# Prompt attention of a hybrid decoder step: scores made as query rows for the maximum and a second time with keys on the partitions for the exponential

## What is computed

```python
s = jnp.einsum('bqhd,bkhd->bhqk', qb, k) * scale
s = s + cq[..., :, None] - ckT[:, :, None, :]
s = jnp.where(kpos <= qpos, s, -jnp.inf)
p = jax.nn.softmax(s, axis=-1)
o = jnp.einsum('bhqk,bkhd->bqhd', p, v)
y = (o * jax.nn.silu(z)) @ w_out
```

## Time and profile before

| what | us |
|---|---|
| median of 3 runs (lowest, highest) | 2239.72 (2234.27, 2247.66) |
| the profiled execution's own time | 2248.77 |
| its span, first to last instruction | 2247.0 |
| first instruction of `attend` | 1391.8 from the span's start |
| first matmul of the output projection | 2116.1 |
| PE busy in the span | 1930.5 (86%) |

### The profile page before, as it was taken

One profiled execution on the slowest core, in us unless ns is written; L12 is line 12 of the kernel. 1 busy time (PEld: TensorE's weight loads), 2 busy tenths in 40 slices (PEclk: granted clock), 3 DMA queues, 4 the chain that ended last, 5 costly groups with the idle time before them and its releaser, 6 DMA issues. The chain is left out here.

```text
span 2247.0 us, 39897 instructions
## 1 busy us (share of the span) xinstructions
PE 1930.5 (86%) x15120; PEld 1416.0 (63%) x15120; DVE 1129.9 (50%) x1810; ACT 563.5 (25%) x1253; POOL 349.8 (16%) x401
## 2 busy tenths in 40 slices
PE   4999999999999788999999996877877768768798
PEld 3876877777787566877877774544444434344475
DVE  4444534544563687677677763333334333333423
ACT  4211121121121421111111111333433334233431
POOL 0000000000000034544445442011011010110010
PEclk9999999999999898999999997568889788687899
DMA  4111111111111479999999997247678676685761
GB/s 136 38 44 48 43 40 56 35 49 47 39 49 38 161 232 308 343 312 341 348 325 330 317 323 253 105 154 248 218 212 258 224 233 225 203 257 181 276 243 71
DMA packets 218393, 413.65 MB, mean 184 GB/s; under 512 B 18593, under 2 KB 129858, under 8 KB 218014
## 3 DMA queue, kind: packets, MB, share of 16 engines
q1 hardware_dynamic: 148764, 222.15, 30.6%
q0 software_dynamic: 51648, 180.71, 23.5%
q10 hardware_dynamic: 17874, 9.27, 1.4%
HBM read 370.85 MB, written 41.94 MB: 184 GB/s over the span
## 5 line engine op out<-in xcount | busy, mean ns | idle before, releaser
L1180 DVE STREAM_TRANSPOSE kt<-k_raw 128x1024 f32<-128x1024 f32 x256 | 310.8, 1234 | 145.7 <-DMA k_raw<-in_cache_k_dram,k_idx 120.0
L347 POOL DMA_INDIRECT k_raw<-in_cache_k_dram,k_idx x256 | 259.4, 1013 | 444.4 <-DVE kt L1180 284.6
L765 PE MATMUL ps_a<-h_hi,w_hi 128*128 128x512 f32 x656 | 265.7, 405 | 1.7 <-DVE w_lo L1017 1.7
L766 PE MATMUL ps_a<-h_lo,w_hi 128*128 128x512 f32 x656 | 258.7, 394 | 0.0
L767 PE MATMUL ps_a<-h_hi,w_lo 128*128 128x512 f32 x656 | 258.6, 394 | 0.0
L1693 DVE TENSOR_REDUCE pp_nm<-ps_a 128x1 f32<-128x128 f32 (+3 forms) x64 | 48.5, 758 | 306.4 <-PE ps_a L1421 306.4
L1017 DVE TENSOR_TENSOR w_lo<-w_raw,w_hi 128x1024 fp32r<-128x1024 f32 x97 | 109.1, 1124 | 171.3 <-ACT w_hi L594 169.0
L1443 PE MATMUL b<-con,p_p 128*128 128x128 f32 x432 | 98.4, 347 | 102.7 <-DVE p_p L1701 48.4
L765 PE MATMUL ps_b<-h_hi,w_hi 128*128 128x512 f32 x384 | 157.2, 409 | 0.0
L766 PE MATMUL ps_b<-h_lo,w_hi 128*128 128x512 f32 x384 | 152.1, 396 | 0.0
L767 PE MATMUL ps_b<-h_hi,w_lo 128*128 128x512 f32 x384 | 152.0, 396 | 0.0
(11 more groups left out here) (291 smaller groups left out, 3131.8 us busy)
## 6 DMA issues: line engine op xcount, KB each, us to landing
v_pg<-in_cache_v_dram SPq DMA_DIRECT2D x256, 512.0 KB, 5.1
w_raw<-in_w_in_pool_dram SPq DMA_DIRECT2D x32, 512.0 KB
w_raw<-in_w_in_attn_dram SPq DMA_DIRECT2D x32, 512.0 KB
w_raw<-in_w_out_pool_dram SPq DMA_DIRECT2D x16, 512.0 KB
s_scr<-ss_st ACTq DMA_DIRECT2D x64, 128.0 KB
s_in<-s_scr POOLq DMA_DIRECT2D x16, 512.0 KB, 5.0
d_sb<-decay POOLq DMA_DIRECT2D x32, 256.0 KB, 6.9
z_scr<-x_st SPq DMA_DIRECT2D x8, 528.0 KB, 4.6
```

The source lines that it names most:

```text
L347: pool.indirect_dma_start(k_raw[:, k, :], None, cache_rows, bass.IndirectOffsetOnAxis(ap=k_idx[:, u, k:k + 1], axis=0)).then_inc(k_full[k] ...
L765: nc.tensor.matmul(ps, ah, bh, start=j == 0, stop=False)
L766: nc.tensor.matmul(ps, ah, bl, start=False, stop=False)
L1180: V.transpose(kt[u % 2][:, :, 32 * k:32 * k + 32], k_raw[:, k, :].rearrange("p (i c) -> p i c", c=32)).then_inc(dve_kt, 1)
```

## The change

It touches `attend`, its buffers, and little else.

- The row maxima of a pair are made ahead of it. `query_rows(b+1, m)` computes the scores as before, for m = 0 to 7, in parts of at most 512 columns, spread over slots 1 to 6 of pair b; DVE takes each part's maximum (`row_max`), then the negated maxima of all 16 blocks in one tile (`max_columns`). PE transposes it (`max_turn`, slot 7), ACT copies it out, and ACT's own queue writes it to DRAM (`nm_d`, 8 KB) and, after that has landed, reads it into row 66 of `qa` (`max_row`). `k_aug` gets a row more that matches it.
- The scores are made a second time with the keys on the partitions: `keys_turned(b, s)`, key block s against all queries from block s on, minus the maximum. They and the row scores go through a ring of four PSUM banks. ACT's exponential writes straight to `pt_x`, two buffers for each head. No block is transposed, and none is normalised.
- `prompt_values` now takes up to 512 columns at a time and adds up all slots in `ps_a`. The sums over the keys are made by DVE (`part_sums`, adds of `pt_x` into `acc`) and by PE (`row_sums`, a matmul with ones, twice a pair). `gate` divides and multiplies twice a pair, 512 columns each.
- In a slot, the values of slot s-1 stand ahead of the turned scores of slot s; then come row scores, the sample's turn, and sample values.
- `qa`, `ka`, `v_pr` have two buffers. The queries, keys and values of pair b+1 are asked for when the turned scores and the values of pair b-1 are done; `score_half` two pairs ahead.
- The sample of pair b is done within pair b. All 8 pairs carry one, and the output projection carries none. Ahead of pair 0 stand its row scores, its sample scores and the first exchange of maxima. `w_o` is asked for early in the last pair.
- The gates are loaded in one transfer after the first sample scores.

The core of the diff:

```diff
+        ring = (ps_b[:, 0:512], ps_b[:, 512:1024], ps_c[:, 0:512], ps_c[:, 512:1024])
+        M_SLOTS = ((), (0, 1), (2,), (3, 4), (5,), (6,), (7,), ())
+        def turned(s):
+            return [(h, a, e) for h in range(2) for a, e in ((P * s, 512), (max(512, P * s), SEQ)) if a < e]
+        def row_parts(m):
+            return [(h, a, e) for h in range(2) for a, e in ((0, min(512, P * m + P)), (512, P * m + P)) if a < e]
...
+                def keys_turned(b, par, s, uses):
                     if s == 0:
-                        pe.wait_ge(ld_qk, b * 32 + 32)
+                        pe.wait_ge(ld_nm, b * 16 + 16)
+                    for i, (h, a, e) in enumerate(turned(s)):
+                        j = uses.index(("t", T_AT[s] + i))
+                        ring_wait(b, uses, j)
+                        diag = a == P * s
+                        out = ring[j % 4]
+                        mm = nc.tensor.matmul(out[:, 0:e - a], ka[par][:, h, P * s:P * s + P], qa[par][:, h, a:e],
+                                              start=True, stop=not diag)
+                        if diag:
+                            mm = nc.tensor.matmul(out[:, 0:P], caus_b[:, :], ident_b[:, :], start=False, stop=True)
+                        mm.then_inc(pe_t, 1)
...
+                def max_turn(b):
+                    pe.wait_ge(dve_nx, b + 1)
+                    pe.wait_ge(dve_s, b * N_S + 5)
+                    nc.tensor.transpose(b6[0:16, 0:P], nm_c[:, :], ident).then_inc(pe_nm, 1)
...
+                    for a, e in ((P * s, 512), (max(512, P * s), SEQ)):
+                        if a < e:
+                            for h in range(2):
+                                r = HD * h
+                                mm = nc.tensor.matmul(o_ps[r:r + HD, a:e], v_pr[par][:, s, r:r + HD], pt_x[h][s % 2][:, a:e],
+                                                      start=s == 0, stop=s == (3 if e == 512 else 7), tile_position=(0, r))
...
+                def pair(b, par, first, last):
+                    uses = USES_LAST if last else USES_ALL
                     for s in range(SLOTS):
                         if s == 0:
-                            scores(b, 0)
+                            if not first:
+                                prompt_values(b - 1, 1 - par, SLOTS - 1)
+                            keys_turned(b, par, 0, uses)
                         else:
-                            prompt_values(b, s - 1)
...
+                            prompt_values(b, par, s - 1)
+                            keys_turned(b, par, s, uses)
+                        if not last:
+                            if s == 1:
+                                pe.wait_ge(ld_qk, b * 32 + 64)
+                            for m in M_SLOTS[s]:
+                                query_rows(b + 1, 1 - par, m, uses)
+                        if s % 2 and s < SLOTS - 1:
+                            sample_turn(b, (s + 1) // 2)
+                        if s == 4:
+                            row_sums(b, 0)
+                        if s == 5:
                             new_turn(b)
...
+                        if s == 6 and not last:
+                            new_scores(b + 1, False)
+                        if s == SLOTS - 1 and not last:
+                            max_turn(b + 1)
+                        sample_values(b, s)
+                        if s == SLOTS - 1 and not last:
+                            sample_turn(b + 1, 0)
+                        if s == 0 and not first:
+                            row_sums(b - 1, 1)
...
+                def max_row(b, par):
+                    act.wait_ge(pe_nm, b + 1)
+                    past(act, ld_nm, b * 16)
+                    nc.scalar.copy(nm_t[:, :], b6[0:16, 0:P]).then_inc(act_nm, 1)
+                    act.wait_ge(act_nm, b + 1)
+                    act.dma_start(nm_d[:, :], nm_t[:, :]).then_inc(st_nm, 16)
+                    act.wait_ge(st_nm, b * 16 + 16)
+                    act.dma_start(qa[par][AUG:AUG + 1, :, :].rearrange("o h t -> o (h t)"),
+                                  nm_d.rearrange("(o j) t -> o (j t)", o=1)).then_inc(ld_nm, 16)
```

More of the change, by code:

```diff
@@ L255, in build @@
         SW = PAST // 4 + TS
[L256 to L262, removed]
+        pt_x = [[place(f"pt_x{h}{i}", [P, SEQ], F32, big_at(2048 * h + 1024 * i)) for i in range(2)] for h in range(2)]
@@ L1254, in t2_uses, with ring_uses @@
+        N_T, N_M = T_AT[SLOTS], M_AT[SLOTS]
+        def ring_uses(rows):
             uses = []
             for s in range(SLOTS):
[L1256 to L1262, removed]
-            return uses
-        y_ps = ((ps_a[:, 0:512], ps_a[:, 512:DM]), (ps_c[:, 512:DM], b7[:, :]))
@@ L1281, in t2_bank @@
[L1281 to L1289 removed]
+                uses += [("t", T_AT[s] + i) for i in range(len(turned(s)))]
@@ new lines, in _ @@
+                for m in range(SLOTS):
+                    query_rows(0, 0, m, ROWS_FIRST)
+                new_scores(0, True)
+                max_turn(0)
+                pe.wait_ge(ld_ls, 16)
+                sample_turn(0, 0)
+                pair(0, 0, True, False)
+                with pe.Fori(0, NB // 2 - 1) as i:
+                    pair(i * 2 + 1, 1, False, False)
+                    pair(i * 2 + 2, 0, False, False)
+                pair(NB - 1, 1, False, True)
+                prompt_values(NB - 1, 1, SLOTS - 1)
@@ L1560, in _ @@
-                    if i == 4:
+                    for k in range(KT8):
+                        if i == 0:
+                            pe.wait_ge(dve_wl, k + 1)
+                        if k == 0:
+                            pe.wait_ge(dve_zl, i + 1)
+                        high, low = z_hi[i % 2][:, k, :], z_lo[:, k, P * i:P * i + P]
+                        for half in range(2):
+                            c = slice(512 * half, 512 * half + 512)
+                            out = y_ps[i % 2][half]
+                            nc.tensor.matmul(out, high, wo_hi[k][:, c], start=k == 0, stop=False)
+                            nc.tensor.matmul(out, high, wo_lo[k][:, c], start=False, stop=False)
+                            mm = nc.tensor.matmul(out, low, wo_hi[k][:, c], start=False, stop=k == KT8 - 1)
@@ new lines, in _ @@
+                V.memset(mx_c[:, :], 2 * NEG).then_inc(dve_z, 1)
+                dve.wait_ge(dve_z, 2)
+                queries(0)
+                for m in range(SLOTS):
+                    row_max(0, m, ROWS_FIRST)
+                max_columns(0)
+                for o in range(4):
+                    sample_scores(0, o, True)
+                new_scores(0)
+                common_max(0)
+                dve.wait_ge(ld_z, 16)
+                pair(0, True, False)
+                with dve.Fori(0, NB // 2 - 1) as i:
+                    pair(i * 2 + 1, False, False)
+                    pair(i * 2 + 2, False, False)
```

620 lines of the change are left out of this document (314 added, 306 removed).

## The result

The changed kernel takes 2316.99 us (median of 4 runs, 2312.17 to 2318.32), the kernel before 2236.99 beside it. The ratio is 1.0348 with a 95% interval of [1.0304, 1.0392]: 3.5% slower, where I had forecast 4.1% faster. The profiled execution took 2312.17 us, 1.7 over its span.

What follows compares the result with a forecast made beforehand. Waits, chiefly the boundary load of ka, and half clock filled 33 of 89.7 us a pair. Work 67.9, exchange 6.1 and clock 3 made 77; with start, last pair, projection and tail, 2148 us after adjustment, range 2080 to 2220.

Steps and rivals of the forecast that it cites:

- first turned scores: Block start until pair 0's turned scores: row scores 26 us, sample scores, exchange; 43.5 us in all, reached at 1435.3.
- seven pairs: The seven pairs after the first turned scores, at 77 us each: 539 us, ending at 1974.3.
- output projection: Projection after the last pair, without the last sample's pages, turns and new tokens: 102.2 us instead of 120.6.
- the load of `ka`: Pair-boundary load of keys, asked for a pair ahead: lands in 15.0 us, needed some 22 us later, so hidden.
- Rival F: Next pair's load requested too late for the double buffer; would have to take 22 us, not 15.0; chance 0.02.
- Rival E: Before a pair's turned scores, the exchange is as slow as the load it replaces: pair 98 us, sum 2315; chance 0.09.
- L: Duration of one leg, write or read, of the exchange of maxima through DRAM; taken as 4.5 us.
- B: Exchange of maxima hidden, leg 2.6 us and no clock restart: pair 70.5 us, about 2100 us; chance 0.20.
- The exchange: Maxima go through DRAM to row 66 of qa before the turned scores; PE stalls 6.1 us a pair.
- The clock: Half clock after gaps in a pair: 2 us for a restart, 1 for late pages, 3 us a pair.
- PE's work, 67.9 us a pair: TensorE work in a pair: 46.5 us kept plus 21.4 added, against 56.5 before.
- A: The forecast as summed: pair 74 to 80 us, total 2127 to 2169 us; chance 0.44.

Runs made afterwards that it cites:

- before67: The kernel before with a 67th row in k_aug and ka loaded as 67 rows in one transfer, scores still using 66: 2401.74 us.
- split67: The changed kernel with the keys of a pair in two transfers, rows 0 to 65 and row 66 alone: 2219.82 us, ratio 0.9893.
- split_gate: split67 with the gate multiplying by z first, which frees the values' bank, and taking the reciprocal afterwards: 2180.12 us, ratio 0.9728.
- gate_unrolled: split_gate with the loop over the middle pairs written out on PE, ACT and DVE: 2173.06 us, ratio 0.9661.
- gate_fill: gate_unrolled with 20 overwritten 128x128 matmuls a pair ahead of PE's wait for row 66 of qa: 2165.91 us, ratio 0.9617.
- rows68: The changed kernel with 68 rows of keys in one transfer, the 68th unused: 2253.95 us.

## Why the prediction was wrong, point by point

The forecast of the end was 2154.6 us in the span, and the measured one is 2310.5. By stations:

| step | forecast | changed kernel |
|---|---|---|
| first turned scores | 1435.3 | 1457.5 |
| seven pairs | 539 | 666.9 |
| last pair and the split of weights and z | 67.8 | 74.5 |
| output projection | 102.2 | 101.8 |
| tail | 10.3 | 9.8 |

- **The step that failed is the load of `ka`.** The text said that it "lands in 15.0 us", and is "needed in slot 1, some 22 us later against 15.0: hidden, with 5 to spare". The 15.0 was measured with 66 rows, and the change loads 67. I took the row more as nothing; it made the landing 43.4 (`before67` 35.2, in a kernel without the rest). `split67` prices it: 97 of the 169 us between 2148 and 2317. In the changed kernel the need came 33 us after the request, not 22, so even twice the 15.0 would have been hidden.
- **Rival F** named this very place and said what it would take: "it would have to take 22". I gave it 0.02, because a row stood for the duration. A changed shape is an operation that the trace does not show, and wanted bounds from both sides.
- **Rival E** had the right number, 98 us a pair and 2315, by the wrong way. Its price was the exchange at L = 15; the last legs measured 4.19 and 4.69 against the 4.5 assumed. Its number is no support for it. (B's pair, 70.5 in the text, is 70.2 by its own formula, 67.9 + 2 x 2.6 - 2.9; nothing hangs on it.)
- **The reciprocal** had no price. "ACT and DVE keep up" was argued from maxima and adds of 0.7 us per 512 columns; a reciprocal of 128x512 takes 3.36 us. DVE's total was no issue (52% of the span); the place was: the reciprocal and two products stood between the last values of a pair and the first of the next. 40 us by `split_gate`.
- **The exchange.** Stall 6.1 us was forecast; PE's wait for row 66 is 4.2 a boundary (29.2 us in seven in `gate_unrolled`). That the price came out near was luck in part: on the chain of `split_gate` the write took 1.3 to 4.4 and the read 6.0 to 8.0, both together 8.3 to 12.0 against the 9.0 assumed. Taking the second leg away was worth 2.3 a pair. The crowd at the boundary was named in the text; that freeing PE there only brings it to the pages was not.
- **The clock.** I gave 2 us for a restart. In `split_gate` the first four turned scores take 7.6 us (1599.77 to 1607.38) against 3.8 in `gate_fill` (1598.97 to 1602.79), so they alone lose 3.8. The direction was right and the size too small, though `gate_fill` shows that little of it comes back. The text also held it possible that the clock rises whatever the gaps do; it doesn't, as `split_gate` has no block transposes and is granted 0.50 behind its gap.
- **PE's work, 67.9 us a pair, was close.** In `gate_fill` the period is 78.1. Without the fill (33.0 us in six periods, 5.5 each) and the waits for pages, ACT, DVE and row 66 (27.8 in six, 4.6 each) it is 68.0. That still has some half clock in it (granted 0.95), so at full clock the work is a few us less than the sum.
- **The turn of the loop** had no term. It held PE 14.8 us in `split_gate`, half of it beside the exchange.
- **Ahead of the first pair**: 13.6 of the 22 us late are the start of the first row scores, 1405.4 instead of 1391.8. In the versions they stood between 1386 and 1398, with the same 12 us of waiting at the head of the block, though nothing that a version changes for speed lies ahead of them; why the changed kernel was later is open. The row scores took 34.3 us instead of 26, nearly all at half clock, within the bounds given.
- **The projection and the tail** came within 0.5 us, as they stood on durations of the same shapes.

With the row by itself and the reciprocal behind, the kernel takes 2180 us, inside the range of 2080 to 2220, 32 above the forecast; its period is 79.5, inside A's 74 to 80. Of the 21.7 us a pair between 77 and 98.7, 12.6 go with the load of `ka`, 6.6 with the reciprocal, and 2.5 are left. That the rest is so near the forecast is partly luck: the turn of the loop and more half clock stand in it, and the exchange cost less than its 6.1. The restructuring does about what was forecast; what wasn't priced took it back and more.

**Open**: what the packets of 4 B are for and what they cost. They come at the load's start (1723 small packets from 1622 to 1626), so they can't be what makes the 35 us after that slow, but the burst and the single engine were not tried apart. Why the form of two heads gets one engine and the form of one head does not is not shown either.

## What to carry to other kernels

The duration of a transfer belongs to its shape, not to its bytes: when a change adds a row to a load, ask what the new count does to how it is dealt out, and compare the landing, the number of packets, and the DMA share while it is under way first of all. Keep slow elementwise work (a reciprocal, here 3.36 us per 512 columns) off the chain that frees a matmul's bank: consume the bank first, divide after. And what is taken off a crowded place is worth only what the next limit leaves: here 130 us of matmuls were worth some 91, and a load put off to spare 14 us of waits cost 21.

## What the runs showed of the hardware

- A load of 67 x 2 rows of 4 KB from POOL's queue landed in 43.4 us (35.2 in `before67`); of 66 x 2 in 7.9 to 15.0; of 68 x 2 in 23.8; of 67 rows twice in 8.5 each. Without pages beside it, it ran at 26 GB/s and 6.4% of 16 engines; beside the pages, both queues together had 28 GB/s at a share of 0.07. Its rows came whole, with 1950 packets more a load, nearly all of 4 B, in a burst at the start. Its issue also held POOL longer. The groups of POOL in the changed kernel and in the kernel before:

```profile
L365 POOL DMA_DIRECT2D ka<-k_aug x8 | 17.4, 2180 | 3.6 <-issue 3.6
```

```profile
L362 POOL DMA_DIRECT2D ka<-k_aug x8 | 6.8, 845 | 2.0 <-issue 2.0
```

- A small write to DRAM and a read of it back into one partition, 8 KB each, took 4.19 and 4.69 us beside 512 KB pages in the changed kernel; the chain of `rows68` has reads of 5.1 to 10.3.
- 4 to 5 us of idle PE at a boundary were followed by some 10 us of work at 1.2 GHz (`split_gate`, granted clock 0.50 from 1599.7 to 1610 behind 4.02 us; `gate_unrolled`, 1680.4 to 1690 behind 5.09); in the changed kernel, with a second wait of 5.13 in it, by some 20. With PE busy in that time, the same matmuls ran at 2.4 GHz (`gate_fill`, 1.00 from 1599 to 1605).
- A reciprocal of 128x512 in fp32 took 3.36 us on DVE, a product of the same shape 0.69.
- PE stood up to 7.8 us at two of the three turns of a loop over pairs (`split_gate`); with the loop written out these pauses were gone.
